# Neighbourhood attention as one block, its bias tables made beside the projection, and the modulation copies of the norms in another order

## The reference

```python
bias = rpb[:, (row_idx - r + NA_KH_MAX - 1)[None, :, None], dc[:, None, :]]
s_loc = einsum('bchd,bcijhd->bhcij', qr, kg) + bias        # 8 x 16 neighbours of each query
s_ctx = einsum('bchd,blhd->bhcl', qr, k_c)                 # and all 256 context keys
p = softmax(concatenate([s_loc, s_ctx], -1))
y = p_loc @ v_neighbours + p_ctx @ v_c
...
m = split(silu(c) @ w_ada + b_ada, 6)                      # shift, scale, gate of both sub-layers
x = layer_norm(DN_ALPHA * x + m[2] * y, ln_g, ln_b)
h = x * (1 + m[4]) + m[3]
```

## Time and profile before

| | us |
|---|---|
| median of 3 runs | 4437.65 (4434.73 to 4438.77) |
| the profiled execution | 4434.96 |
| its span, first to last instruction | 4433.3 |
| PE busy / PEld / DVE / ACT / POOL | 3759.7 / 3016.2 / 1810.2 / 1059.4 / 239.8 |
| mean granted clock of TensorE | 0.916 |

### The profile page before, as it was taken

The page is one execution under the profiler, slowest core; times in us unless marked ns, Lnnn a source line. Parts: engine busy times, 40 slices in busy tenths (PEclk is TensorE's granted clock), DMA queues, the critical chain, the costliest instruction groups (busy, mean ns, idle before and its releaser), DMA issues. The chain is left out here.

```text
span 4433.3 us, 53015 instructions
## 1 busy us (share of the span) xinstructions
PE 3759.7 (85%) x22306; PEld 3016.2 (68%) x22306; DVE 1810.2 (41%) x2051; ACT 1059.4 (24%) x1443; POOL 239.8 (5%) x138
## 2 busy tenths in 40 slices
PE   3999467939795999999998699567939869999997
PEld 2888345418684888888886588445428658888886
DVE  3111667545524222332333321567647443333334
ACT  1000332515514111111112300232416241111113
POOL 2000003002100000000000000002003000000000
PEclk7999779968897999999999799779969989999998
DMA  5332532041132111011102332331041302111111
GB/s 183 84 85 71 184 113 49 7 104 39 38 113 76 53 43 43 28 42 38 34 28 82 95 92 87 120 111 41 10 100 36 128 24 57 43 43 57 43 43 43
DMA packets 296559, 300.50 MB, mean 68 GB/s; under 512 B 42095, under 2 KB 265947, under 8 KB 296155
## 3 DMA queue, kind: packets, MB, share of 16 engines
q1 hardware_dynamic: 270778, 249.34, 19.1%
q0 software_dynamic: 6912, 30.15, 2.2%
q10 hardware_dynamic: 18720, 18.88, 1.3%
HBM read 238.74 MB, written 62.55 MB: 68 GB/s over the span
## 5 line engine op out<-in xcount | busy, mean ns | idle before, releaser
L485 PE MATMUL psum<-h_hi,f_whi 128*128 128x512 f32 (+1 forms) x1760 | 481.7, 371 | 46.2 <-DVE f_wlo L1020 46.2
L485 PE MATMUL psum<-h_lo,f_whi 128*128 128x512 f32 (+1 forms) x1760 | 480.8, 371 | 0.0
L485 PE MATMUL psum<-h_hi,f_wlo 128*128 128x512 f32 (+1 forms) x1760 | 480.8, 371 | 0.0
L485 PE MATMUL psum<-h_hi,w_hi 128*128 128x512 f32 (+1 forms) x1392 | 369.3, 368 | 98.7 <-DVE w_lo L546 67.1
L485 PEld LDWEIGHTS psum<-h_hi,f_whi 128*128 128x128 f32 x1760 | 308.5, 188 | 105.4 <-DVE f_wlo L1020 46.7
L485 PE MATMUL psum<-h_lo,w_hi 128*128 128x512 f32 (+1 forms) x1392 | 366.6, 366 | 0.0
L485 PE MATMUL psum<-h_hi,w_lo 128*128 128x512 f32 (+1 forms) x1392 | 366.5, 366 | 0.0
L1026 DVE SCALAR_TENSOR_TENSOR y<-psum,mods,y 128x1024 f32<-128x1024 f32 (+1 forms) x264 | 260.4, 1014 | 258.6 <-PE psum L485 257.7
L485 PEld LDWEIGHTS psum<-h_lo,f_whi 128*128 128x128 f32 x1760 | 308.3, 188 | 58.9
L485 PEld LDWEIGHTS psum<-h_hi,f_wlo 128*128 128x128 f32 x1760 | 308.1, 188 | 58.8
L485 PEld LDWEIGHTS psum<-h_hi,w_hi 128*128 128x128 f32 x1392 | 239.9, 190 | 146.0 <-issue 39.8
(11 more groups left out here) (271 smaller groups left out, 5255.9 us busy)
## 6 DMA issues: line engine op xcount, KB each, us to landing
f_raw<-in_w_ffn_in SPq DMA_DIRECT2D x88, 512.0 KB, 5.3
ada_w<-in_w_ada SPq DMA_DIRECT2D x30, 1024.0 KB, 10.1
w_raw<-in_w_in SPq DMA_DIRECT2D x48, 512.0 KB, 5.3
proj_cm<-lin_stage POOLq DMA_DIRECT2D x38, 640.0 KB, 4.2
f_raw<-in_w_ffn_out SPq DMA_DIRECT2D x44, 512.0 KB, 3.7
ada_w<-in_w_ada ACTq DMA_DIRECT2D x18, 1024.0 KB, 6.9
att_raw<-proj_cm SPq DMA_DIRECT2D x48, 320.0 KB, 5.8
hg_pj<-proj_cm SPq DMA_DIRECT2D x20, 640.0 KB, 9.0
```

What stands on the lines that cost most here:

```text
L485: ins = nc.tensor.matmul(out[:, t0:t0 + tn], w, h[:, t0:t0 + tn], start=start and n == 0, stop=stop and n == 2)
```

## The change

1. `load_blocks`, `na_prepare` and `attention` are replaced by one block, `na_attention`, written out over 6 heads without a `Fori`. SyncE issues head 0's four loads, the three V blocks, the table of head 0, then head and table of each next one. TensorE turns V in the same block (four tiles, `scores(0)`, six tiles, `scores(1)`), and ScalarE copies it, ahead of its first `probs`.
2. Scores lie in two sets of two banks, turned probabilities in two banks, results in two banks. The bias is added to the local columns in place in PSUM; the copy of the context columns is gone, and maximum and exponential read PSUM. `product` waits for the result of tile n - 2. GpSimd no longer copies V.
3. ScalarE stages the next head in one piece, after the second tile of a head.
4. The output uses both PSUM sets in turn, and ScalarE copies the middle block.
5. The bias tables are built inside `linear` by a class `BiasTables`: steps on SyncE between the first weight loads, twelve masks on VectorE before the last evacuation, six stores to a new DRAM tensor `na_bias_masked`. `na_attention` loads a head's table (128 x 1472) back, in two buffers.
6. In `residual_norm` ScalarE's two `mod_copy` calls of a round are moved behind `modulated` and behind `new_x`.

```diff
@@ BiasTables, new @@
+    def load(self, sp):
+        a = self.k.a
+        sp.dma_start(self.colm[:], a["c_colmask"]).then_inc(self.s_m.h, 16)
+        sp.dma_start(self.midm[:], a["c_midmask"].rearrange("p (s c) -> p s c", s=MID)).then_inc(self.s_m.h, 16)
+        sp.wait_ge(self.s_z.h, self.s_z.at(1))
+        mid = GRID_W - 1 - (NA_KW - 1)
+        sp.dma_start(self.rows[:, mid:mid + 2 * NA_KW - 1], a["na_rpb"][self.l].rearrange("h r c -> (h r) c")).then_inc(self.s_r.h, 16)
...
+    def spread(self, sp):
+        sp.wait_ge(self.s_sk.h, self.s_sk.at(16))
+        for h in range(6):
+            for par in range(2):
+                src = self.k.rpb_skew[h * 15 + 1 - par:h * 15 + 1 - par + SLOTS].rearrange("s c j -> c s j")
+                sp.dma_start(self.table[par * GRID_W:(par + 1) * GRID_W, h, 0:SLOTS], src).then_inc(self.s_b.h, 16)
+
+    def mask(self, dve):
+        nc, t = self.k.nc, self.table
+        dve.wait_ge(self.s_m.h, self.s_m.at(32))
+        dve.wait_ge(self.s_b.h, self.s_b.at(12 * 16))
+        for h in range(6):
+            nc.vector.tensor_tensor(t[:, h, 0:SLOTS], t[:, h, 0:SLOTS], self.colm[:].unsqueeze(1).to_broadcast([P, SLOTS, GRID_W]),
+                                    ALU.add).then_inc(self.s_cm.h, 1)
+            dve.wait_ge(self.s_cm.h, self.s_cm.at(h + 1))
+            nc.vector.tensor_tensor(t[:, h, SLOTS:SLOTS + MID], t[:, h, 2:2 + MID], self.midm[:], ALU.add).then_inc(self.s_mid.h, 1)
+
+    def store(self, sp):
+        for h in range(6):
+            sp.wait_ge(self.s_mid.h, self.s_mid.at(h + 1))
+            sp.dma_start(self.k.bias_dram[:, h], self.table[:, h].rearrange("p s c -> p (s c)")).then_inc(self.s_st.h, 16)
+        sp.wait_ge(self.s_st.h, self.s_st.at(6 * 16))
@@ linear, SyncE @@
-                in_turn(sp, units, load)
+                bias.load(sp)
+                load(0, 0, 0)
+                load(1, 1, 0)
+                bias.pad(sp)
+                load(2, 0, 1)
+                bias.skew(sp)
+                load(3, 1, 1)
+                bias.spread(sp)
...
+                bias.store(sp)
@@ linear, VectorE @@
                 for u in range(2 if widths else (units - 2) // 2 * 2, units):
+                    if u == units - 1:
+                        bias.mask(dve)
                     evac(u, u % 2)
@@ residual_norm, ScalarE @@
                         root(i)
-                        mod_copy(2 * i)
...
                             modulated(i - 1)
+                    if i < n_c:
+                        mod_copy(2 * i)
                     if i + 1 < n_c:
                         square(i + 1)
-                    if i < n_c:
-                        mod_copy(2 * i + 1)
                     if i >= 1 and not last:
                         upper(i - 1)
                         new_x(i - 1, XA, s_xa)
+                    if i < n_c:
+                        mod_copy(2 * i + 1)
@@ na_attention, new @@
+        def score(n):
+            return k.psum[:, 2 * (n % 2):2 * (n % 2) + 2].rearrange("p a b -> p (a b)")
+
+        def turned(x):
+            return k.psum[:, 4 + x % 2]
+
+        def out(n):
+            return k.psum[:, 6 + n % 2, 0:HD]
...
+                head(0)
+                for i in range(3):
+                    sp.dma_start(vraw[:, i], k.pj_dram[:, V_BLOCK + i]).then_inc(s_vl.h, 16)
+                bias(0)
+                for h in range(1, HEADS):
+                    head(h)
+                    bias(h)
...
+                pe.wait_ge(s_vl.h, s_vl.at(48))
+                for t in range(4):
+                    values(t)
+                scores(0)
+                for t in range(4, TT):
+                    values(t)
+                scores(1)
...
+                stage(0)
+                for t in range(TT):
+                    act.wait_ge(s_vt.h, s_vt.at(t + 1))
+                    nc.scalar.copy(v6[:, t], turned(t)[:, 0:3 * P]).then_inc(s_v.h, 1)
+                probs(0)
+                for n in range(N):
+                    xs = of_tile[n]
+                    copy(xs[0])
+                    if n + 1 < N:
+                        probs(n + 1)
+                    for x in xs[1:]:
+                        copy(x)
+                    if n % n_t == 1 and n // n_t + 1 < HEADS:
+                        stage(n // n_t + 1)
...
+                        nc.vector.tensor_tensor(score(n)[:, 0:local], score(n)[:, 0:local], bt[:, h % 2, slot * GRID_W:slot * GRID_W + local],
+                                                ALU.add).then_inc(s_b.h, 1)
```

More of the change, by code:

```diff
@@ L87, in __init__ @@
         self.spare = []
+        self.made = 0
         sb, dram = self.sb, self.dram
@@ L586, in linear @@
         x.done(units + 2)
+    bias.done()
 def streams(tokens):
@@ L1161, in attention @@
     n_g = len(groups)
-    assert n_t % 2 == 0 and n_g % 2 == 0
-    of_tile = [[x for x in range(n_g) if groups[x][0] == n] for n in range(n_t)]
-    n_q = max(t[0] for t in tiles) + 1
-    copier = ["act", "act" if bias is not None else "dve"]
-    stage_at = 1
+    of_tile = [[x for x in range(n_g) if groups[x][0] == n] for n in range(N)]
+    biased = [sum(tiles[i % n_t][3] is not None for i in range(n + 1)) for n in range(N)]
     def width(t):
         return t[1][-1][0] + t[1][-1][2]
+    wide = max(width(t) for t in tiles)
@@ L1200, in attention @@
-        o_ps = k.psum[:, 6, 0:HD]
-        def blocks(e, body):
-            with e.Fori(0, 2) as b:
-                body(b, False)
-            body(2, True)
-        def staging(b, n, last, stage):
-            part = n % (n_t // 2) - stage_at
-            if part in (0, 1) and n < n_t // 2:
-                stage(b, 1, part)
-            elif part in (0, 1) and not last:
-                stage(b + 1, 0, part)
+        sem = k.stage_sems(st)
+        vraw = k.sb(st, "na_v_raw", [P, 3, NT])
+        v6 = k.sb(st, "na_v", [P, TT, 3 * P])
@@ L1301, in product @@
                     for i, (_, rows, tile) in enumerate(keys):
[L1302 removed]
+                        ins = nc.tensor.matmul(out(n), pt[0:rows, x % 2, i * P:(i + 1) * P], v6[0:rows, tile, h * HD:(h + 1) * HD],
                                                start=x == of_tile[n][0] and i == 0, stop=x == of_tile[n][-1] and i == len(keys) - 1)
                     ins.then_inc(s_pv.h, 1)
[L1306 to L1316 removed]
@@ L1317, in _ @@
-                scores(0, 0)
-                scores(0, 1)
-                blocks(pe, body)
-                pe.wait_ge(s_o.h, s_o.at(2 + 3 * n_t))
+                pe.wait_ge(s_vl.h, s_vl.at(48))
[5 more added lines that the diff above has]
+                scores(1)
+                pe.wait_ge(s_v.h, s_v.at(TT))
+                for x in range(n_g):
+                    n = groups[x][0]
+                    turn(x)
+                    if x == of_tile[n][0] and n + 2 < N:
+                        scores(n + 2)
+                    if x:
+                        product(x - 1)
@@ new lines, in _ @@
+                probs(0)
+                for n in range(N):
+                    xs = of_tile[n]
[6 more added lines that the diff above has]
+                        stage(n // n_t + 1)
+                act.wait_ge(s_yt.h, s_yt.at(2))
+                nc.scalar.copy(yb[:, 1], y_banks(1)).then_inc(s_ya.h, 1)
@@ new lines, in _ @@
+                negmax(0)
+                negmax(1)
+                for n in range(N):
+                    inverse(n)
+                    if n + 2 < N:
+                        negmax(n + 2)
+                    result(n)
+                for b in (0, 2):
+                    dve.wait_ge(s_yt.h, s_yt.at(b + 1))
+                    nc.vector.tensor_copy(yb[:, b], y_banks(b)).then_inc(s_yd.h, 1)
+    for s in range(2):
+        s_raw[s].done(3 * 64)
+        s_bl[s].done(3 * 16)
+    s_vl.done(48)
@@ L1455, in gqa_attention @@
+    for x in (s_vt, s_v):
+        x.done(TT)
+    for x in (s_hi, s_lo):
+        x.done(HEADS)
+    s_qs.done(HEADS - 1)
+    for x in (s_s, s_nb, s_p, s_ri, s_o):
+        x.done(N)
+    s_b.done(biased[-1])
+    for x in (s_t, s_pt, s_pv):
+        x.done(n_g)
+    s_yt.done(3)
+    s_yd.done(2)
+    s_ya.done(1)
+    s_st.done(48)
 def gqa_attention(k, ctx, v2):
@@ L2541, in hgrn @@
     s_yd.done(16 * len(groups))
-def load_blocks(k, dst, first):
-    n = dst.shape[1]
-    s = k.sem("blocks_loaded")
-    with k.nc.Block() as block:
-        @block.sync
-        def _(sp):
-            for i in range(n):
-                sp.dma_start(dst[:, i], k.pj_dram[:, first + i]).then_inc(s.h, 16)
-            sp.wait_ge(s.h, s.at(16 * n))
-    s.done(16 * n)
 def project_in(k, l, h_hi, h_lo):
```

450 lines of the change are left out of this document (171 added, 279 removed).

## The result

The changed kernel takes 4270.93 us (median of 4 runs, 4269.08 to 4281.59); beside it the kernel before took 4436.19 us. The ratio is 0.9632, 95% interval 0.9615 to 0.965: 165 us or 3.7% less, where 141 us were forecast (4295, range 4259 to 4338). The profiled execution has a span of 4267.2 us, 166.1 less than before, and a mean granted clock of 0.929 instead of 0.916.

The account below looks back on a forecast made before the run. TensorE paces the attention loop, a serial chain its start, ScalarE layer 0's norms. Start -93, loop -18, tail -6, norms -29, projection +5 sum to -141 us: forecast 4295 us, range 4259 to 4338 (the sum's own 4270 to 4316).

Parts of the forecast that it names:

- NA start: Start of neighbourhood attention: bias chain and one set of barriers go, first turn at 23.4 us; 93 us saved in all.
- the bounds, -102 and -85: Start of neighbourhood attention: gain of 102 us if V were free, 85 if loads and V add up in full.
- NA loop: Query-tile loop of neighbourhood attention, both layers: two result banks remove waits, staging gives some back; about -18 us.
- its terms, -28, -2 and +13: Attention loop: -28 us for result waits removed, -2 for the context copy dropped, +13 for staging in one piece.
- its own bound of -33: Attention loop: -33 us if the staging is absorbed, plus the addressing of the old `Fori`.
- NA tail: End of neighbourhood attention: one copy and one wait for it go; 6 us saved in all, 3 to 8.
- Norms: Two norms of layer 0: cast and new x run under the variance; 29 us saved in all, bounds 15 and 39.
- Projection: Projection, both layers: small loads delay the first product, table transfers and masks are covered; +5 us, 2 to 12.
- The clock: Rival, attention loop: staging waits lower TensorE's clock at each of ten head changes, adding 40 us: 4335; chance 0.12.
- The tables: Rival, projection: mask outlasts the last unit or stores outlast the stage, up to 21 us a layer, 4337; chance 0.04.
- The in-place chain: Slower rival, attention loop: add, maximum, softmax, turn, scores outlast two TensorE tiles; 4440 us or more; chance 0.03.
- the extra price of adding in place: Attention loop, VectorE writing PSUM: between nothing and about 0.7 us a tile, hidden under TensorE; taken as 0.

Follow-up runs that it names:

- before, written out: The kernel before with its attention block's loop over three pairs of heads written out, order of work unchanged: 4429.19 us, ratio 0.9987.
- the square first: The changed kernel with the next chunk's square ahead of the modulation on ScalarE in the norms, second modulation copy after the next root: 4247.85 us, ratio 0.9568.
- the weights first: The changed kernel with the projection's first two weight loads issued before the three small loads of the tables: 4269.78 us, ratio 0.9608.

## Why the prediction was right, and which term was off

**NA start, right.** -96.6 for -93. V landed at 12.9 to 13.2 us for 13.5, the ten V tiles with the scores between took some 7.5 us for 8.5. Of the bounds, -102 and -85, the first was the nearer; V in fact cost only 2.6 to 2.8 us over the old start of 18.9.

**NA loop, right in sign, mis-sized: -34 for -18** (its terms, -28, -2 and +13, give -17). This is the term of the sum that was off, and just outside its own bound of -33. It put down the removed waits and the staging as two amounts that add up, -14 and +6.5 in each layer, and everything else in layer 1 at nothing. For layer 1, where the clock is full, three kernels stand between before and after:

| us, loop of layer 1 | loop | step | put down |
|---|---|---|---|
| before | 160.3 | | |
| before, written out | 156.2 | -4.1 | 0, named in the bound only |
| changed, one result bank | 159.0 | +2.8 | 0 |
| changed | 145.4 | -13.5 | -14 + 6.5 |

So three things were off. The addresses were seen but stood only in the outer bound; the row for them was there, since the last pair of heads has tiles of 3.38 us. Bank and staging together gave 13.5 and not 7.5: the wait that the bank removes is 17.1 us in this kernel, and the staging takes 3.7 of them (five tiles of 4.02 for 3.29) and not 6.5. The prediction had 1.3 us a head change for 0.73: the copy came some 1.4 us late, not 1.8, and TensorE had more to do meanwhile. Third, the changed kernel with one bank is 2.8 us slower than the old one written out, although it has dropped a copy worth 1.1: its steady tile lasts 3.45 us against 3.38, and VectorE starts the result 0.07 us later in it. No term stood for that, and no experiment takes it apart.

In layer 0 the same steps are -9.0, -7.8 and -2.4, with a clock of 0.92, 0.94, 1.00 and 0.93 in the four kernels, so no step there is the price of one edit. What can be said is where the 19.2 us came from: 4.0 at the head changes (59.8 us in the fifteen tiles there before, 55.7 after), 15.2 in the other tiles.

**NA tail, right in mechanism**, with 8.9 for 6 just beyond its upper bound of 8. Layer 1 gave 3.2 for 3. Layer 0 gave 5.7, and there the clock took part: TensorE turned the rounds at 0.50 before (1198 to 1207) and at 1.00 now (1128 to 1132).

**Norms, right.** -27.8 for -29, and +28.6 in the stages when undone. The period is 13.6 us for 14. That ScalarE's order still left the variance waiting for the square behind the modulation was not in the prediction; the runs with the square first took 22 us more out of the same two norms.

**Projection, right.** +4.9 for +5, and for the reason given: the small loads. The Sync queue's hold, the masks and the stores of the tables were covered; the masks with 1.8 us to spare, and paid for in full beyond that.

**The sum.** 4434.96 less 141 is 4294, but with the 2.7 us of the median it is 4296.7 and not 4295. The start gave 3.6 us more than forecast, the tail 2.9, the loop 16 and the untouched stages 3.6: two thirds of the 24 us between 4295 and 4271 are the loop. No large errors cancelled between the stages; inside the loop the 2.8 us stood against the other two.

**The rivals.** The clock did not fall at each head change: the staging waits of 0.7 us left layer 1 at 1.00. The low stretches of layer 0 are the old ones, at the wait for the first softmax of a head. The tables were hidden. The in-place chain was no bound. The prediction put the extra price of adding in place between nothing and 0.7 us, and it is nothing; each maximum over PSUM takes 0.96 and 1.02 us, as the earlier trace rows have it from SBUF. The adds before and after and the maximum after (ns, least, median, greatest):

```profile
L1393 DVE TENSOR_TENSOR att_s<-psum,na_bias x96: 679/724/759, 993.4 to 3458.5; 128x512 f32<-128x512 f32 x48, 128x576 f32<-128x576 f32 x48
...
L1458 DVE TENSOR_TENSOR psum<-psum,na_bias x96: 678/723/767, 942.4 to 3293.5; 128x512 f32<-128x512 f32 x48, 128x576 f32<-128x576 f32 x48
...
L1463 DVE TENSOR_REDUCE na_negmax<-psum x108: 404/958/1026, 943.1 to 3294.2; 128x1 f32<-128x768 f32 x48, 128x1 f32<-128x832 f32 x48, 128x1 f32<-128x256 f32 x12
```

By the larger fixed term for PSUM in the Trainium skill ("VectorE: DVE Perf Modes", the TRN2 errata) each maximum would be 0.065 us longer, an estimate; here the rows differ by 0.01 us at most.

## What to carry to other kernels

When a loop with register addresses has a last turn that is written out, compare a tile of each in the trace: the difference belongs in the sum, not in its bounds, and it is to be asked which wait it stands in, since another edit may take the same wait out. A cost can be hidden behind a wait that the same change removes: the staging cost nothing with one result bank and 0.73 us a head with two. Prices got by undoing one edit each don't add up where this is so; a row of kernels that differ by one edit does. On an engine that works through a list by itself, put what only feeds a later stage behind what starts the slow step of another engine: moving a square, a copy and a subtraction, with no work removed, gave 36 us here (26 and 10). Short tiles at the end of a group leave the next group's first chain uncovered; spreading them out took 12 us off the loop of layer 0.

## What the runs showed of the hardware that was not expected

- The same wait of 1.76 us on TensorE was followed by a granted clock of 0.62 over 9 us at one head change and of 1.00 at the next, and the same pattern came in three traces (the changed kernel twice, and with the weights first). With the same attention code behind other norms or masks the pattern was another, and the loop 176.4 to 180.4 us long. So the length of the wait alone does not decide it; what else does is open.
- With 17 us of short waits in the loop (one result bank) the clock was 1.00 throughout, so that the kernel with less idle time had the lower clock. This is one trace.
- VectorE adds in place in PSUM at the pace of the old add into SBUF: 0.68 us for 512 columns and 0.75 for 576, where it was 0.69 and 0.76.
- A tile inside the `Fori`, with addresses and wait values in registers, lasted 0.11 us longer (some 24 matmuls, 1156 in layer 1's 48 tiles) while TensorE set the pace; three quarters of it stood in TensorE's wait for VectorE's result.
